# A decoder step on one core: the S5 taps go to scratch and back in four large transfers, ScalarE masks them all, and the mixer's written order is changed

## The reference

```
u = proj[..., :512]                       # 32 groups of 16 channels
bu = einsum('btgc,gpc->btgp', u, bbar)    # complex, 64 states per group
x  = associative_scan(a, bu)              # h[t] = a*h[t-1] + bu[t]
y  = real(einsum('gcp,btgp->btgc', c, x)) + d*u
z  = gelu(y);  out = z * sigmoid(z @ glu_w + glu_b)
```

## Time and profile before

| | |
|---|---|
| median of 3 runs | 1459.41 us (1457.45 to 1460.13) |
| the profiled execution | 1459.49 us, of which the span is 1457.7 us |
| granted TensorE clock, mean | 0.981 of full speed |
| TensorE busy | 1369.6 us (94%) |
| VectorE busy | 444.9 us (31%) |
| ScalarE busy | 253.7 us (17%) |
| GpSimd busy | 55.4 us (4%) |
| transfers | 471.84 MB, 324 GB/s over the span |

### The profile page before, as it was taken

One profiled execution on the slowest core, in us unless ns is written; L12 is line 12 of the kernel. 1 busy time (PEld: TensorE's weight loads), 2 busy tenths in 40 slices (PEclk: granted clock), 3 DMA queues, 4 the chain that ended last, 5 costly groups with the idle time before them and its releaser, 6 DMA issues.

```text
span 1457.7 us, 21163 instructions
## 1 busy us (share of the span) xinstructions
PE 1369.6 (94%) x8649; PEld 695.7 (48%) x8649; DVE 444.9 (31%) x881; ACT 253.7 (17%) x480; POOL 55.4 (4%) x111
## 2 busy tenths in 40 slices
PE   8958999999999999999999999998998999988997
PEld 5735688866665633434334343343343433433442
DVE  5699846434121321312112111121121111311112
ACT  3223431212223212101101011011010110110102
POOL 4233000000000000000000000000000000000000
PEclk9978999999999999999999999999999999999999
DMA  8960121013939769999999999999999999999994
GB/s 325 203 116 30 62 91 60 32 60 120 388 135 410 279 252 397 401 423 428 427 428 428 428 428 428 428 428 428 428 428 428 428 428 428 428 429 425 428 426 179
DMA packets 43335, 471.84 MB, mean 324 GB/s; under 512 B 4992, under 2 KB 10368, under 8 KB 11520
## 3 DMA queue, kind: packets, MB, share of 16 engines
q1 hardware_dynamic: 37264, 461.42, 76.4%
q10 hardware_dynamic: 6000, 9.41, 3.3%
HBM read 465.33 MB, written 5.48 MB: 323 GB/s over the span
## 4 chain that ended last, share of the span: by engine, by line
PE 71%; DMA 20%; DVE 7%; issue 1%; ACT 1%; ACTq 0%; SPq 0%; DVEq 0%
DMA big<-in_w_gu 18%; PE bank L1189 16%; PE bank L1238 14%; PE bank L716 10%; PE bank L1112 5%; PE bank L979 2%; PE bank L799 2%; PE bank L1302 2%; PE bank L1258 2%; DMA big<-u_windows 2%; PE bank L898 1%; PE bank L1119 1%; PE bank L1214 1%; PE bank L1287 1%; DVE big L1847 1%
## 5 line engine op out<-in xcount | busy, mean ns | idle before, releaser
L1189 PE MATMUL bank<-big 128*64 128x512 f32 x1920 | 427.9, 603 | 27.6 <-DMA big<-in_w_gu 27.4
L1189 PEld LDWEIGHTS bank<-big 128*64 128x64 f32 x1920 | 147.1, 138 | 305.3 <-issue 295.0
L1238 PE MATMUL bank<-big 128*64 128x512 f32 x960 | 209.4, 594 | 0.0
L716 PE MATMUL bank<-big 128*128 128x320 f32 (+1 forms) x688 | 187.5, 430 | 9.1 <-DVE big L1922 6.8
L716 PEld LDWEIGHTS bank<-big 128*128 128x128 f32 x688 | 130.1, 191 | 63.0 <-issue 13.4
L2242 DVE TENSOR_TENSOR big<-big,bank 128x320 f32<-128x320 f32 x120 | 58.6, 488 | 303.0 <-PE bank L1258 297.8
L2228 DVE TENSOR_SCALAR big<-bank 128x512 f32<-128x512 f32 x32 | 22.2, 693 | 391.5 <-PE bank L1189 361.3
L1238 PEld LDWEIGHTS bank<-big 128*64 128x64 f32 x960 | 70.2, 137 | 127.9 <-issue 126.0
L1593 ACT ACTIVATE big<-big 128x512 f32<-128x512 f32 x30 | 18.8, 626 | 448.4 <-DVE big L2228 448.4
L1353 ACT ACTIVATE big<-bank 128x320 f32<-128x320 f32 (+3 forms) x122 | 53.1, 436 | 232.7 <-PE bank L716 41.9
L1112 PE MATMUL bank<-big 128*128 128x512 f32 x192 | 87.1, 603 | 1.4 <-DVE big L2176 1.4
(11 more groups left out here) (408 smaller groups left out, 1146.5 us busy)
## 6 DMA issues: line engine op xcount, KB each, us to landing
big<-in_w_gu SPq DMA_DIRECT2D x128, 2048.0 KB, 25.1
big<-in_w_down SPq DMA_DIRECT2D x62, 2048.0 KB, 22.3
big<-in_dense SPq DMA_DIRECT2D x47, 1024.0 KB, 8.4
big<-u_windows ACTq DMA_DIRECT2D x32, 160.0 KB, 10.4
big<-in_w_down SPq DMA_DIRECT2D x4, 1024.0 KB, 20.8
big<-in_smw SPq DMA_DIRECT2D x1, 1408.0 KB, 19.3
big<-in_xT SPq DMA_DIRECT2D x2, 640.0 KB, 4.6
big<-in_consts SPq DMA_DIRECT2D x1, 1028.5 KB, 14.5
```

Of the source, the lines that this page charges most:

```text
L716: last = mm(b[:, 0:n], w[:, k, :], src[:, k, :], start=(k == 0), stop=(k == kt - 1))
L1189: last = mm(ps[n][part, :], xte[:, 2 * j + k, part], w[s][:, k, n * 512:n * 512 + 512], start=False, stop=end)
L1238: last = mm(ps[bank][part, :], actT[:, 4 * d + i, part], w[s][:, i, h * 512:h * 512 + 512], start=(d == 0 and i == 0), stop=end)
```

## The change

The scratch tensor gets rows of 320 words without the seven words of padding, and one more row in front, whose last seven words are set to zero by a small transfer of their own. The rows of u are stored by one transfer for each tile, and in another order: the eight groups of one channel number stand behind each other. So the taps of one tile can be read with one transfer of 128 pieces of 10,240 bytes. What a piece reads before the start of a group is the end of another group; the masks, which every tile gets, set it to zero. All four masks are done by ScalarE in seven instructions each, and stand further ahead of the tile's `blk` than before. The loads of tiles 0 and 1 leave the list: tile 0 is loaded after the squares of the memory tokens, tile 1 at "memsum". `u_rows(1)` moves ahead of the eight `n1` products. `MIX_ORDER` is written anew. From `lora_down` on it is as before.

```diff
-MIX_ORDER = [("in", "k0"), ("memsum", 0), ("load", 0), ("in", "k1"), ("f", 0), ("in", "k2"), ("load", 1), ("c", 0), ("in", "k3"),
-             ("par", 0), ("memtotal", 0), ("in", "z0"), ("f", 1), ("in", "z1"), ("win", 0), ("win", 1), ("blk", 0), ("memroot", 0), ("load", 2), ("scan", 0),
-             ("y", 0), ("in", "z2"), ("mix", "k"), ("par", 1), ("in", "z3"), ("out", 0), ("c", 1), ("blk", 1), ("load", 3),
-             ("gelu", 0), ("scan", 1), ("gated", 0), ("y", 1), ("in", "r0"), ("win", 2), ("delta", "z"), ("in", "r1"), ("shares", 0),
-             ("shares", 1), ("out", 1), ("par", 2), ("c", 2), ("in", "r2"), ("blk", 2), ("scan", 2), ("y", 2), ("win", 3), ("gelu", 1), ("gated", 1),
-             ("shares", 2), ("in", "r3"), ("in", "v0"), ("mix", "r"), ("out", 2), ("par", 3), ("in", "v1"), ("c", 3), ("gelu", 2), ("gated", 2),
-             ("blk", 3), ("scan", 3), ("y", 3), ("lora_up", 0), ("in", "v2"), ("in", "v3"), ("kk", 0), ("memnorm", 0), ("out", 3),
-             ("gelu", 3), ("mix", "v"), ("gated", 3), ("lora_down", 0), ...
+MIX_ORDER = [("in", "k0"), ("memsum", 0), ("win", 0), ("in", "k1"), ("f", 0), ("in", "k2"), ("win", 1), ("c", 0), ("in", "k3"),
+             ("par", 0), ("memtotal", 0), ("in", "z0"), ("f", 1), ("blk", 0), ("load", 2), ("memroot", 0), ("par", 1), ("scan", 0), ("y", 0),
+             ("in", "z1"), ("mix", "k"), ("blk", 1), ("load", 3), ("out", 0), ("scan", 1), ("y", 1), ("win", 2), ("in", "z2"), ("c", 1),
+             ("win", 3), ("in", "z3"), ("out", 1), ("par", 2), ("gelu", 0), ("gated", 0), ("c", 2), ("in", "r0"), ("delta", "z"),
+             ("blk", 2), ("scan", 2), ("y", 2), ("gelu", 1), ("in", "r1"), ("shares", 0), ("gated", 1), ("out", 2), ("par", 3), ("in", "r2"),
+             ("shares", 1), ("shares", 2), ("gelu", 2), ("c", 3), ("gated", 2), ("blk", 3), ("scan", 3), ("y", 3), ("in", "r3"), ("in", "v0"),
+             ("out", 3), ("mix", "r"), ("lora_up", 0), ("in", "v1"), ("memnorm", 0), ("in", "v2"), ("in", "v3"), ("kk", 0), ("gelu", 3),
+             ("mix", "v"), ("gated", 3), ("lora_down", 0), ...
...
-        u_dram = nc.dram_tensor("u_windows", [W5, T + 7], F32)
+        u_dram = nc.dram_tensor("u_windows", [W5 + 1, T], F32)
...
-                if ct < 2:
-                    pe.wait_ge(S("uwin"), ct + 1)
-                else:
-                    pe.wait_ge(S("uwin_places"), (BL - 1) * (ct - 1))
+                pe.wait_ge(S("uwin"), (BL - 1) * (ct + 1))
...
+            def store_rows(ct):
+                stored(act, f"u{ct}")
+                to = bass.AP(u_dram, T + ct * P * T, [[T, 8], [8 * T, GC], [1, T]])
+                act.dma_start(to, uT[:, ct, 7:]).then_inc(S(f"u_stored{ct}"), 16)
+
+            def load_windows(ct):
+                if ct >= 2:
+                    computed(act, f"loc{ct - 2}")
+                act.wait_ge(S(f"u_stored{ct}"), 16)
+                act.wait_ge(S(f"u_stored{ct - 1}" if ct else "front_stored"), 16)
+                src = bass.AP(u_dram, T + ct * P * T - 7, [[1, BL], [8 * T, GC], [1, 8 * T]])
+                act.dma_start(uwins[ct % 2].rearrange("p g t -> p (g t)"), src).then_inc(S(f"uwin_in{ct % 2}"), 16)
+
+            act.wait_ge(S("u_pad"), 1)
+            act.dma_start(bass.AP(u_dram, T - 7, [[7, 1], [1, 7]]), uT[0:1, 0, 0:7]).then_inc(S("front_stored"), 16)
+            store_rows(0)
+            store_rows(1)
             act.wait_ge(S("mem_in"), 16)
             for k in range(KT):
                 step(af(memsq[:, k, :], memT[:, k, :], ACT.Square), "memsq")
-            stored(act, "u3")
-            act.wait_ge(S("u_pad"), 1)
-            act.dma_start(u_dram.ap().rearrange("(c p) t -> p c t", p=P), uT).then_inc(S("u_stored"), 16)
+            load_windows(0)
+            store_rows(2)
+            store_rows(3)
...
-            act.wait_ge(S("u_stored"), 16)
...
-                elif kind == "win" and n >= 2:
+                elif kind == "win":
                     mask_windows(n)
                 elif kind == "memsum":
                     norm_parts(rm, "m")
+                    load_windows(1)
...
             u_rows(0)
+            u_rows(1)
             for k in range(KT):
                 step(tt(n1[:, k, :], xg[:, k, :], rx, mul), "n1")
-            u_rows(1)
...
-            def mask_windows(ct):
-                dve.wait_ge(S(f"uwin_in{ct % 2}"), 16 * BL * (ct // 2 + 1))
-                step(tt(uwins[ct % 2], uwins[ct % 2], over(con("window"), 1, 8), mul), "uwin")
...
-                elif kind == "win" and n < 2:
-                    mask_windows(n)
```

More of the change, by code:

```diff
@@ L180 @@
 IN_ORDER = "kzrv"
-MIX_ORDER = [("in", "k0"), ("memsum", 0), ("load", 0), ("in", "k1"), ("f", 0), ("in", "k2"), ("load", 1), ("c", 0), ("in", "k3"),
-             ("par", 0), ("memtotal", 0), ("in", "z0"), ("f", 1), ("in", "z1"), ("win", 0), ("win", 1), ("blk", 0), ("memroot", 0), ("load", 2), ("scan", 0),
-             ("y", 0), ("in", "z2"), ("mix", "k"), ("par", 1), ("in", "z3"), ("out", 0), ("c", 1), ("blk", 1), ("load", 3),
-             ("gelu", 0), ("scan", 1), ("gated", 0), ("y", 1), ("in", "r0"), ("win", 2), ("delta", "z"), ("in", "r1"), ("shares", 0),
-             ("shares", 1), ("out", 1), ("par", 2), ("c", 2), ("in", "r2"), ("blk", 2), ("scan", 2), ("y", 2), ("win", 3), ("gelu", 1), ("gated", 1),
-             ("shares", 2), ("in", "r3"), ("in", "v0"), ("mix", "r"), ("out", 2), ("par", 3), ("in", "v1"), ("c", 3), ("gelu", 2), ("gated", 2),
-             ("blk", 3), ("scan", 3), ("y", 3), ("lora_up", 0), ("in", "v2"), ("in", "v3"), ("kk", 0), ("memnorm", 0), ("out", 3),
-             ("gelu", 3), ("mix", "v"), ("gated", 3), ("lora_down", 0), ("knorm", 0), ("decays", 0), ("memk", 0), ("decay_exp", 0),
-             ("memk", 1), ("memk", 2), ("memk", 3), ("memk", 4), ("memk", 5), ("glu", 0)]
@@ new lines @@
+MIX_ORDER = [("in", "k0"), ("memsum", 0), ("win", 0), ("in", "k1"), ("f", 0), ("in", "k2"), ("win", 1), ("c", 0), ("in", "k3"),
[5 more added lines that the diff above has]
+             ("out", 3), ("mix", "r"), ("lora_up", 0), ("in", "v1"), ("memnorm", 0), ("in", "v2"), ("in", "v3"), ("kk", 0), ("gelu", 3),
+             ("mix", "v"), ("gated", 3), ("lora_down", 0), ("knorm", 0), ("decays", 0), ("memk", 0), ("decay_exp", 0), ("memk", 1),
+             ("memk", 2), ("memk", 3), ("memk", 4), ("memk", 5), ("glu", 0)]
@@ L1401, in s5_params @@
                 step.read_out(af(dst[:, :, 1, 16:32], b[:, :, 16:32], ACT.Identity), f"kk{ct}")
-            def load_windows(ct):
-                if ct >= 2:
-                    computed(act, f"loc{ct - 2}")
-                for tap in range(BL):
-                    src = bass.AP(u_dram, ct * P * (T + 7) + tap, [[T + 7, GC], [GC * (T + 7), 8], [1, T]])
-                    act.dma_start(uwins[ct % 2][tap * GC:(tap + 1) * GC], src).then_inc(S(f"uwin_in{ct % 2}"), 16)
             def mask_windows(ct):
-                act.wait_ge(S(f"uwin_in{ct % 2}"), 16 * BL * (ct // 2 + 1))
+                act.wait_ge(S(f"uwin_in{ct % 2}"), 16 * (ct // 2 + 1))
                 w = uwins[ct % 2].rearrange("p g t -> p (g t)")
                 for j in range(BL - 1):
-                    step(af(w[:, j::BL], w[:, j::BL], ACT.Identity, scale=con("window")[:, j:j + 1]), "uwin_places")
-            act.wait_ge(S("u_stored"), 16)
+                    step(af(w[:, j::BL], w[:, j::BL], ACT.Identity, scale=con("window")[:, j:j + 1]), "uwin")
             act.wait_ge(S("consts_in"), 16)
```

## The result

The changed kernel takes 1478.69 us (median of 4 runs, 1476.03 to 1482.57), the kernel before took 1459.77 us beside it (4 runs, 1457.45 to 1463.21): a ratio of 1.013, interval 1.0099 to 1.016. It is slower by 19 us. The profiled execution of the changed kernel took 1478.34 us with a span of 1476.5 us.

What follows compares the result with a forecast made beforehand. VectorE's order of work was taken to set TensorE's stalls before 210 us, which move the end. Waits 8.1 us less plus clock 1.6 us less gave 9.7 us off 1459.5 us: 1449.8 us, range 1444 to 1458 us.

Steps and rivals of the forecast that it cites:

- The price of the tap load: Each tile's single 1.31 MB tap load was taken to need 8 us.
- The walk: Step-by-step timing of the new order on TensorE and VectorE up to `out 3`; TensorE's waits fall from 25.8 to 17.7 us.
- the gain of 9.7 us: Whole kernel: 8.1 us less waiting of TensorE plus 1.6 us less lost to low clock.
- The bounds of 6, 12 and 22 us: Tap load: 6 us at mean rate, 12 us at the short pieces' rate, 22 us if also half the engines.
- Half the engines: Tap load: the skill's rule gives 8 engines of 16; at its rate 5.7 us, leaving the sum unchanged.
- the two doubts, rate and engines: Tap load: late taps need both low rate and half the engines, giving 22 us to landing.
- late taps: Rival: taps landing after 22 us delay ScalarE's masks and `par 0` copies, `blk 0` loses 10.7 us; 1463.5 us, chance 0.07.
- the wait for the tanh: VectorE waits 5.1 us for ScalarE's tanh of tile 0, which stands behind its copies of `par 2`.
- Stores: ScalarE's wait for its first store of u's rows to land was given until 27.5 us.
- the mark: Start of the memory-key projections after `knorm`; `knorm` was to end some 10 us earlier than 174 us.
- the wait before `out 1`: TensorE waits for VectorE's `c 1` from 76.6 to 83.9 us, 7.3 us.
- The clock: TensorE's low clock behind stalls: 5.4 us before, two stalls at 1.9 us after, 1.6 us less.

Runs made afterwards that it cites:

- after: The changed kernel itself, one tap transfer a tile with slowest dimension 8, against the kernel before; 1478.69 us, ratio 1.013.
- e9: Changed kernel with tap loads read from the experts' weights, each byte once, the taps' blocks set apart by a gap; 1471.97 us, one run.
- e14: Changed kernel with each tile's tap load cut into four transfers of 32 partitions, slowest dimension still 8; 1461.33 us, one run.
- e1: Changed kernel with eight tap transfers of 16 pieces for each tile in place of one; 1468.42 us, ratio 1.0058.
- e2: Changed kernel with the channel outermost in its one tap transfer (slowest dimension 16), F's columns and masks following; 1457.32 us, ratio 0.9974.
- e13: e1 with each transfer's 16 rows landing 8 partitions apart, F's columns and masks following as in e2; 1460.78 us, ratio 1.0.
- e5: e2 with taps read from the experts' weights, each byte once, rows end to end; 1456.55 us, one run.
- e6: Changed kernel with taps read from the experts' weights, each byte once, rows end to end; 1447.74 us, one run.
- e4: Changed kernel's new order and masks with the old tap loads, eight transfers of 1280-byte pieces a tile; 1469.27 us, ratio 1.0048.
- e7: Kernel before, keeping its order and division of masks, with stores by tile and e2's tap load and F columns; 1453.32 us, ratio 0.9954.
- e8: e2 with `gelu 0` moved ahead of `par 2`, so ScalarE does tile 0's tanh before those copies; 1453.29 us, ratio 0.9954.
- e11: e8 with F computed channel by channel, written without a stride; 1454.53 us, ratio 0.9952.
- e12: e7 with F computed channel by channel, written without a stride; 1452.72 us, ratio 0.9936.
- e10: Changed kernel with the same tap pattern, eight readings of the same 160 KB, laid over the experts' weights; 1477.16 us, one run.
- e3: Changed kernel with taps shifted by 128 bytes each in place of one word, 224 zero words in front; 1476.22 us, one run.

## Why the prediction was wrong, by its own steps

**The price of the tap load.** This is the step that failed: "I take 8 us, nearer to the quick end, since the bytes go to all 128 partitions in long runs like the weights'." Measured were 17.7, 33.6, 16.5 and 20.0 us from issue to mask, and each time it was the transfer that ended ScalarE's wait. The walk hid 12 us at most, so with these numbers the gain of 9.7 us became a loss of 18.8 us in the span. The bounds of 6, 12 and 22 us held three of the four loads; the fourth, tile 1's, was issued 3 us behind tile 0's and ran beside it and the weights. The prediction priced each load alone.

That the bytes go to all 128 partitions is true of the whole and not of any moment. The rates by form (starts of the engines' blocks, if the rows of a transfer are dealt out in order, which the trace does not show engine by engine):

| | engines | start of their rows | GB/s | GB/s for each |
|---|---|---|---|---|
| after, e9 | 8 | 16 partitions apart | 111 to 125 | 14 to 15 |
| e14 | 8 | 4 apart | 188 to 215 | 24 to 26 |
| e1 | 16 | 1 apart, in 16 partitions | 126 to 164 | 8 to 9 |
| e2, e13 | 16 | 8 apart | 210 to 246 | 14 to 16 |
| e5, e6 | 16 | rows end to end | 391 to 408 | 25 |

The loads of e1 and e13 differ in the partitions alone. So it is shown that which partitions a transfer's rows go to, side by side, sets the rate, here by a factor of 1.5 (164 to 246 GB/s). After and e14 differ in this and in the number of transfers. e14's gain, from 113 to 188 GB/s, fits, and e1 shows that cutting a load up does not make it quick by itself; but no run cuts after's load up and leaves its partitions. Why the partitions matter is not seen in a trace. The Trainium skill (SBUF — State Buffer, Door 1: The DMA port swizzle (why `[64,N]` ≈ `[32,N]`)) has a mechanism: partitions belong to 16 ports, and partitions 32 apart, like the four neighbours of an aligned group, share one. By its formula blocks that start 16 partitions apart meet in 4 ports at a time, e1's 16 neighbours in 4, starts 8 apart in 8, e14's in 8. The order of the rates agrees with it, with 28 to 41 GB/s a port in the first kind and 24 to 31 in the second. The spread does not: e1's 41 and after's 28 should be alike, and e1's eight transfers, in part under way together, may reach more ports than the four of one. The page speaks of the partitions of a whole transfer; that it holds for those written at one time, and that rows are dealt out by blocks, are my readings and stay unshown. So does the step from e2's 210 to 246 GB/s to e5's 391: the rows there lie end to end, and each byte is read once, and no run has one without the other at 16 engines.

**Half the engines.** The prediction weighed a rule of the Trainium skill (DMA: Bandwidth & Descriptors, Why a DMA increments its semaphore by 16 and not by 1): 8 engines for a slowest dimension of 8. The trace agrees, with a DMA share of 0.46 to 0.55 and 8 packets fewer for each load. The prediction left it out of the sum, for half of the engines at the page's rate would have been quick enough. It took the two doubts, rate and engines, as separate accidents that must both come true; here they had one origin, the form of one transfer.

**The rival "late taps"** (1463.5 us) was the mechanism: masks late, the copies of `par 0` behind them, `blk 0` waiting. It had `blk 0` lose 10.7 us with 22 us to landing for each tile, and got 21.5 us. "It decides from about 18 us on" was right in kind: e2, with 10.7 and 16.5 us from issue to mask, is about even with before, the changed kernel with 17.7 and 33.6 us is slower. Its price missed tile 1's 33.6 us, the wait for the tanh behind late masks (12.3 us for 5.1), and two waits inside a job, 6.3 us in `z2` and 1.6 us in `out 2`, which no step had.

**Stores.** "I give it until 27.5 us" for the first store to land; the load behind it was issued at 30.4 us, 3 us late.

**The walk of the new order** was right where the taps are early, as e6 shows: `out 2` begins at 110.05 us (forecast 110.3) after a wait of 9.4 (9.2), `out 3` at 133.07 (133.1) after 1.0 (1.2), the tanh is waited for for 5.1 us (5.1), and the mark is 10.9 us early (some 10). Only the wait before `out 1` was 3.1 us for 7.3; 2.3 us were spent inside `z2` instead. e6's one run took 1447.7 us, 2.1 us less than the 1449.8 forecast. That is luck in part: the walk knew no stop inside `out 2`, ten of the thirteen kernels in the new order have it, and with it the time would be some 1452 us.

**The clock.** Two stalls at half clock were forecast and there are more; behind the long one the stretch from 60 to 66 us has a granted clock of 0.50, which is 1.2 GHz. The step was sound and its stalls were others.

**The new order as a cause.** With the old short pieces (e4) it costs 8.3 us over before; with e2's loads it gains 3.6 us where the old order gains 6.7 us (e2, e7), and with the tanh moved ahead it is level with it (e8). So the gain there is to have comes from quick loads, and the new order on its own adds a demand on them.

**Versions that beat both kernels** are e7, e8, e11 and e12, by 0.5 to 0.6%, and e2 by 0.26%. The first four can't be told apart. e8's profiled execution, without the stop like e6's, has its mark 1.9 us behind e6's. F's stride and the rate of the loads are against e8 and the moved tanh is for it; no run measures them apart.

**Open** stays what holds TensorE inside a job. In the new order it stops after the first products of `z2`, for 6.3 us in the changed kernel and 2.2 us in e2, and between the products of `out 2`, for 1.6 and 1.4 us. In both kernels a packet of the instruction queue falls 1.6 to 3.8 us ahead of each resumption (between 95 and 96 us before 98.2 us, between 72 and 73 us before 74.6 us in e2), so instructions that arrive late would fit. Tap loads can hold them back in `z2` at most: around e2's stop in `out 2`, from 114 to 118 us, the DMA share is 0.02. And e6 and e8 have such a packet 2 to 3 us behind the start of `out 2` and no stop. No run tested it.

## What to carry to other kernels

Price a transfer by its form: the slowest dimension, once dimensions that run into one another are taken as one, gives the engines, and the partitions that its rows go to side by side go into what each of them moves. Here a gap between blocks of 16 rows alone was a factor of 3.5 (118 GB/s in e9 against 408 in e6), with 128 pieces of 10 KB from the same tensor to the same partitions. Move a wait ahead in an engine's queue only when what it waits for is early by its measured time in the crowd, not alone: two loads issued 3 us apart cost 17.7 and 33.6 us. And when an experiment is to change one thing of a transfer, look at its packets and its DMA share first: e6 changed the place and the number of engines. And when two kernels are compared by one profiled execution each, look for a stop that only one of them has: here it was worth 4 us, more than the edit.

## What the runs showed of the hardware

- The partitions written side by side: 164 to 246 GB/s by the stride of the rows' partitions alone (e1, e13), 113 to 188 GB/s with eight engines, where the load is also cut in four (after, e14).
- A source whose dimensions run into one another is dealt out as one: slowest dimension written as 8, 16 engines used, 408 GB/s (e6); a gap between the blocks brings 8 engines and 118 GB/s (e9).
- The packets of a queue count the engines: each transfer has one packet more for each engine that takes part (1954, 1986, 2050 and 2434 packets).
- Reading the same 160 KB eight times over (e10) took 1477.16 us against 1471.97 us with each byte once (e9), one run each, at 8 engines and some 120 GB/s. Shifts of 4 and of 128 bytes are alike (e3, one run).
- On VectorE most of the 128 x 512 products with a stride of 8 words in their output took 1.08 us for 0.69; with the stride in an input 1.02 to 1.05 us.
- A stop of 1.1 to 1.6 us inside a job at half clock cost 3.4 to 4.6 us by the mark, since the clock of 0.50 lasts longer behind it (e2: 0.72 from 126 to 130 us and 1.00 from 130 us; e6, without a stop: 0.78 from 113 to 117 us and 1.00 from 117 us).
